# Layer B of a hybrid decoder step: decay rows by a transfer, keys and values turned by VectorE and five transfers instead of TensorE

## The reference, cut to what matters

```python
gc = jnp.cumsum(to_chunks(g, C, N), axis=-1)              # decay logs
diff = gc[..., :, None] - gc[..., None, :]
decay = jnp.where(tri, jnp.exp(jnp.where(tri, diff, 0.0)), 0.0)
kb = kc * bc[..., None]
lmat = jnp.where(strict, jnp.einsum('nbhik,nbhjk->nbhij', kb, kc) * decay, 0.0)
rhs = jnp.concatenate([vc * bc[..., None], kb * jnp.exp(gc)[..., None]], axis=-1)
sol = lax.linalg.triangular_solve(lmat, rhs, left_side=True, lower=True, unit_diagonal=True)
u, w = sol[..., :dv], sol[..., dv:]
aqk = jnp.einsum('nbhik,nbhjk->nbhij', qc, kc) * decay
kdec = kc * jnp.exp(g_last[..., None] - gc)[..., None]

def step(S, xs):
    u_i, w_i, aqk_i, qg_i, kdec_i, gl_i = xs
    v_new = u_i - jnp.einsum('bhck,bhkv->bhcv', w_i, S)
    o_i = jnp.einsum('bhck,bhkv->bhcv', qg_i, S) + jnp.einsum('bhij,bhjv->bhiv', aqk_i, v_new)
    S = S * jnp.exp(gl_i)[..., None, None] + jnp.einsum('bhck,bhcv->bhkv', kdec_i, v_new)
    return S, o_i
```

## Time and profile before

| | before |
|---|---|
| median of 3 runs | 2109.37 us |
| the profiled execution, time | 2113.68 us |
| the profiled execution, span | 2111.6 us |
| mean granted clock of TensorE | 0.993 |
| TensorE busy | 2072.5 us |
| VectorE busy | 997.2 us |
| ScalarE busy | 697.7 us |
| GpSimd busy | 454.6 us |
| bytes moved by DMA | 210.34 MB |

### The profile page before, as it was taken

How to read it: one execution, slowest core, us unless ns; L and a number is a source line. 1 busy time by engine, 2 the same in 40 slices (tenths; PEclk the granted TensorE clock), 3 DMA queues, 4 the chain that set the end, 5 groups by cost and what they waited for, 6 DMA issues and landing times. The chain is left out here.

```text
span 2111.6 us, 36594 instructions
## 1 busy us (share of the span) xinstructions
PE 2072.5 (98%) x14446; PEld 1487.2 (70%) x14446; DVE 997.2 (47%) x2664; ACT 697.7 (33%) x1631; POOL 454.6 (22%) x639
## 2 busy tenths in 40 slices
PE   8999999999999999999999999999999999999998
PEld 6888888888888887555466777767666666665444
DVE  5234354354435345331238777777876133332252
ACT  4121321322131122231135555555564344532101
POOL 0522232222223213300023134322331200020000
PEclk9999999999999999999999999999998999999999
DMA  7411301211131127668412122222210461134451
GB/s 235 161 43 41 107 27 51 80 41 43 41 97 37 50 83 223 237 202 255 131 31 74 73 95 83 93 87 82 73 48 13 137 256 31 41 105 134 134 161 50
DMA packets 210238, 210.34 MB, mean 100 GB/s; under 512 B 14261, under 2 KB 181653, under 8 KB 209150
## 3 DMA queue, kind: packets, MB, share of 16 engines
q1 hardware_dynamic: 198070, 148.27, 23.7%
q0 software_dynamic: 12000, 59.73, 7.4%
HBM read 179.56 MB, written 68.23 MB: 117 GB/s over the span
## 5 line engine op out<-in xcount | busy, mean ns | idle before, releaser
L887 PE MATMUL bank<-arena 128*128 128x256 f32 (+1 forms) x2688 | 631.7, 386 | 0.0
L887 PEld LDWEIGHTS bank<-arena 128*128 128x128 f32 x2688 | 494.5, 190 | 75.3
L2104 PE MATMUL bank<-arena 128*128 128x352 f32 x1296 | 452.5, 470 | 0.1
L2104 PEld LDWEIGHTS bank<-arena 128*128 128x128 f32 x1296 | 220.8, 191 | 71.4 <-issue 1.0
L2909 PE MATMUL bank<-arena 128*128 128x352 f32 x576 | 176.4, 459 | 0.0
L3399 PE MATMUL bank<-arena 128*128 128x512 f32 x360 | 167.5, 599 | 0.0
L2162 PEld LDWEIGHTS bank<-arena 128*128 128x128 f32 x864 | 129.9, 194 | 45.7 <-DVE arena L2646 3.7
L2909 PEld LDWEIGHTS bank<-arena 128*128 128x128 f32 x576 | 106.6, 190 | 53.3
L1341 POOL TENSOR_TENSOR arena<-arena 128x272 f32<-128x272 f32 (+1 forms) x48 | 31.5, 656 | 507.4 <-ACT arena L1061 487.4
L2162 PE MATMUL bank<-arena 128*128 128x128 f32 x864 | 135.0, 280 | 1.5 <-DVE arena L2646 1.0
L1323 POOL TENSOR_TENSOR arena<-arena 128x512 f32<-128x512 f32 x96 | 122.8, 1279 | 11.3 <-POOL arena L1323 0.9
(11 more groups left out here) (432 smaller groups left out, 2754.1 us busy)
## 6 DMA issues: line engine op xcount, KB each, us to landing
arena<-in_w_in_a SPq DMA_DIRECT2D x48, 512.0 KB, 5.2
arena<-in_w_in_b SPq DMA_DIRECT2D x40, 512.0 KB, 7.5
arena<-in_cache_win_k SPq DMA_DIRECT2D x48, 256.0 KB, 6.1
arena<-in_cache_win_v SPq DMA_DIRECT2D x48, 256.0 KB, 4.7
out<-arena SPq DMA_DIRECT2D x40, 256.0 KB, 3.4
arena<-in_w_mem_kv SPq DMA_DIRECT2D x16, 512.0 KB, 8.1
arena<-in_cache_mem_k SPq DMA_DIRECT2D x32, 256.0 KB, 4.3
arena<-in_cache_mem_v SPq DMA_DIRECT2D x32, 256.0 KB, 4.2
```

Source lines behind the costliest of these rows:

```text
L887: m = nc.tensor.matmul(o[:, 0:hi - lo], w, y, start=k == 0 and i in (0, 1, 3, 5), stop=k == KH - 1, skip_group_check=i in (2, 4, 6))
L2104: m = nc.tensor.matmul(bank[j % 3][:, 0:PART], ring.slots[:, (B1 + b) % RING, k, :], part_in(k, part_), start=k == 0, stop=k == KD - 1)
```

## The change

It takes three kinds of transposition off TensorE.

- **Decay rows.** Ahead of the loop TensorE turns all 64 columns of decay logs once (`decay_rows`), VectorE copies the result, and SP stores it in DRAM (`gc_kept`). For each group but the first SP loads its four rows from there, broadcast to all partitions, an iteration ahead into a buffer of their own (`rows_to`). VectorE adds the mask from there in slot 5 (`mask_rows`).
- **Keys and values.** In slots 6 and 7 VectorE turns the keys and values of group G + 1 in 32x32 blocks in SBUF (`kv_turned`). One transfer puts both into DRAM, four bring them back with the blocks in their final places (`turned_away`, `turned_back`). ScalarE scales them into `kdec` and `vb` in slots 8 to 11 of the next iteration, two activations per chunk (`scale_turned`; slots 5 to 8 for the last group).
- **Order.** `PREP` loses `ra`, `kt` and `vt`; SP's list is written per iteration; iteration 15 has its 20 units later. The `Chain` semaphores, so far never freed, are now freed at the end of each phase.

```diff
+    turned_kept = dram("turned_kept", [2, P, 1024])
+    gc_kept = dram("gc_kept", [64, P])
...
+    gc_rows = r_sb[0:64, 1, :]
...
+    turned_in = [brT[:, HB - 2, 0:1024]] * (2 * HB - 1) + [xpad[:, 0, 0:1024]]
+    turned_kv = [w.rearrange("p (b i c x) -> p b i c x", b=4, i=2, c=4) for w in turned_in]
+    kv_words = sb[:, ZM[0]:ZM[0] + 1024]
+    kv_back = kv_words.rearrange("p (a i c x) -> p a i c x", a=4, i=2, c=4)
+    rows_of = [sb[:, MQ[0]:MQ[0] + 512]] * (2 * HB - 1) + [xpad[:, 1, 0:512]]
...
-    PREP = {5: ("ra",), 7: ("kt",), 8: ("kk",), 9: ("qk",), 15: ("vt",)}
-    NEXT = ("ra", "kk", "qk")
+    PREP = {8: ("kk",), 9: ("qk",)}
+    NEXT = ("kk", "qk")
+    AT_MASK = 5
...
+    AT_TURN = {6: 0, 7: 1}
+    scale_at = lambda G: 5 if G == 2 * HB - 1 else 8
...
-    slots += [[(0, 1)] * 16, [(0, 2)] * 4 + [(0, 1)] * 12]
+    slots += [[(0, 1)] * 16, [(0, 0)] + [(0, 1)] * 10 + [(0, 2)] * 5]
...
+        def rows_to(g):
+            h, c0 = g // 2, GR[g % 2][0]
+            sp.wait_ge(rows_away, 16)
+            after(sp, masked, g - 1)
+            if g == NG_ - 1:
+                sp.wait_ge(cvd, 3 * NG_)
+                sp.wait_ge(tap, 3 * (NG_ - 2))
+            src = gc_kept.rearrange("(c h) i -> h c i", h=HB)[h, c0:c0 + 4]
+            sp.dma_start(rows_of[g], src.unsqueeze(0).to_broadcast([P, 4, P])).then_inc(rows_in, 16)
+        def turned_away(g):
+            sp.wait_ge(turnd, 2 * (g + 1))
+            sp.dma_start(turned_kept[g % 2], turned_in[g]).then_inc(kv_away, 16)
+        def turned_back(g):
+            sp.wait_ge(kv_away, 16 * (g + 1))
+            after(sp, kvs, 4 * g)
+            src = turned_kept[g % 2].rearrange("(a y) (b m) -> b y a m", a=4, b=4)
+            for b in range(4):
+                sp.dma_start(kv_words[quarter(b)].rearrange("p (a m) -> p a m", a=4), src[b]).then_inc(kv_in, 16)
...
+        for G in range(NG_):
+            if G % 2 and G < NG_ - 1:
+                weights(3 * (G // 2) + 8)
+                weights(3 * (G // 2) + 9)
+            if G + 2 < NG_:
+                rows_to(G + 2)
+            if G + 1 < NG_:
+                turned_away(G + 1)
+                turned_back(G + 1)
+            if G % 2 == 0:
+                weights(3 * (G // 2) + 7)
...
-                readout(pe, g, f"ks{c}" if c else "vt")
+                if c:
+                    readout(pe, g, f"ks{c}")
+                else:
+                    pe.wait_ge(kvs, 4 * g + 1)
...
+                pe.wait_ge(kvs, 4 * g + cl + 1)
...
+        def scale_turned(g, cl):
+            w, c = hd[:, g // 2 % 2], GR[g % 2][0] + cl
+            if not cl:
+                act.wait_ge(kv_in, 64 * (g + 1))
+                act.wait_ge(hdv, 3 * g + 3)
+                if g > 1:
+                    left(act, g - 2, f"su{GR[g % 2][1] - 1}")
+            wide = lambda v: v.rearrange("p (a x) -> p a x", x=32)
+            nc.scalar.activation(wide(kdec[:, c, :]), kv_back[:, :, 0, cl, :], ACT.Copy, scale=w[:, KD_, c:c + 1])
+            nc.scalar.activation(wide(vb[:, c, :]), kv_back[:, :, 1, cl, :], ACT.Copy,
+                                 scale=w[:, KN, c:c + 1]).then_inc(kvs, 1)
...
-            elif name == "kt":
-                dve.wait_ge(hdv, 3 * G + 3)
-                nc.vector.tensor_tensor(kdec[:, cs, :], bk(b), factors_of[:, KD_, cs].unsqueeze(2)
-                                        .to_broadcast([P, 4, P]), ALU.mult).then_inc(rd_dve, 1)
-            elif name == "vt":
-                nc.vector.tensor_tensor(vb[:, cs, :], bk(b), factors_of[:, KN, cs].unsqueeze(2)
-                                        .to_broadcast([P, 4, P]), ALU.mult).then_inc(rd_dve, 1)
+        def kv_turned(G, i):
+            h, gr = G // 2, G % 2
+            dve.wait_ge(sild, 3 * G + 2 + i)
+            if G and not i:
+                dve.wait_ge(kv_away, 16 * G)
...
+            x = qkvT[:, h % 2, 1 + i, gr * 512:(gr + 1) * 512].rearrange("p (c b x) -> p c b x", c=4, b=4)
+            nc.vector.transpose(turned_kv[G][:, :, i].rearrange("p b c x -> p c b x"), x).then_inc(turnd, 1)
+        def mask_rows(G):
+            dve.wait_ge(rows_in, 16 * G)
+            if G > 2:
+                left(dve, G - 3, f"av{GR[(G - 3) % 2][1] - 1}")
+            nc.vector.tensor_tensor(ATs[G % 3], rows_of[G], wide4(mat(M_GE)), ALU.add).then_inc(masked, 1)
```

More of the change, by code:

```diff
@@ L525, in _ @@
     def _(dve):
-        own = Chain(nc, dve, "in_dve")
+        own = Chain(sem, dve, "in_dve")
         def norm(n):
@@ L1130, in _ @@
     def _(dve):
-        own = Chain(nc, dve, "dve_a")
+        own = Chain(sem, dve, "dve_a")
         def evacuate(t, i):
@@ L1300, in _ @@
     def _(pool):
-        own = Chain(nc, pool, "pool_a")
+        own = Chain(sem, pool, "pool_a")
         def weight_sums(pair, ns):
@@ L1747, in _ @@
     def _(dve):
-        own = Chain(nc, dve, "wa_dve")
+        own = Chain(sem, dve, "wa_dve")
         def add(n, half):
@@ L2078, in state_away, with weights @@
             sp.dma_start(p_delta[0, 0, h], S_of(h, NT)).then_inc(s_out, 16)
-        for b in range(3 * HB):
+        def rows_to(g):
[16 more added lines that the diff above has]
+                sp.dma_start(kv_words[quarter(b)].rearrange("p (a m) -> p a m", a=4), src[b]).then_inc(kv_in, 16)
+        def weights(b):
             if b % 3 == 2 and b // 3 >= 3:
@@ L2082, in _ @@
             ring.load(sp, B1 + b + 1)
-        state_away(HB - 3)
-        ring.load(sp, B2 + RING)
+        for b in range(7):
+            weights(b)
+        readout(sp, 0, "gr")
+        sp.dma_start(gc_kept, gc_rows).then_inc(rows_away, 16)
+        rows_to(1)
+        turned_away(0)
+        turned_back(0)
+        for G in range(NG_):
[9 more added lines that the diff above has]
+                weights(3 * (G // 2) + 7)
         state_away(HB - 2)
@@ L2313, in gate_piece @@
                 act.wait_ge(ring.used, B2 + i + 1)
+            if i == 0 and part_ == 0:
+                act.wait_ge(masked, NG_ - 2)
+            if i == 1 and part_ == 0:
+                act.wait_ge(kvs, 4 * NG_)
             if i == 2 and part_ == 0:
@@ L2379, in exps @@
         def exps(G):
-            readout(act, G, "ra")
+            if G:
+                act.wait_ge(masked, G)
+            else:
+                readout(act, 0, "ra")
             act.wait_ge(hdv, 3 * G + 2)
@@ L2489, in _ @@
     def _(dve):
-        own = Chain(nc, dve, "b_dve")
+        own = Chain(sem, dve, "b_dve")
         stepped = [0]
@@ L2735, in _ @@
         turned(0, "qk")
+        kv_turned(0, 0)
+        kv_turned(0, 1)
         for w in range(CW):
@@ L2742, in _ @@
             for s in SLOTS:
+                if s == AT_MASK and G + 1 < NG_:
+                    mask_rows(G + 1)
                 if G < NG_:
@@ L2746, in _ @@
                     chunk_step(G - 1, s)
+                if s in AT_TURN and G + 1 < NG_:
+                    kv_turned(G + 1, AT_TURN[s])
                 if s == AT_INV:
@@ L2772, in _ @@
     def _(pool):
-        own = Chain(nc, pool, "b_pool")
+        own = Chain(sem, pool, "b_pool")
         def prefix(h, i):
@@ L3009, in _ @@
     def _(dve):
-        own = Chain(nc, dve, "m_dve")
+        own = Chain(sem, dve, "m_dve")
         def conv_turned(t):
@@ L3487, in _ @@
     def _(act):
-        own = Chain(nc, act, "d_act_own")
+        own = Chain(sem, act, "d_act_own")
         def squared(o):
@@ L3558, in _ @@
     def _(dve):
-        own = Chain(nc, dve, "wb_dve")
+        own = Chain(sem, dve, "wb_dve")
         gt2 = lambda v: v[:, 64:66].unsqueeze(2)
```

33 lines of the change are left out of this document (23 added, 10 removed).

## The result

The changed kernel takes 2274.43 us (median of 4 runs, 2271.98 to 2277.12), the kernel before 2111.76 in the same session (4 runs): ratio 1.077, 95% interval 1.075 to 1.080, 163 us slower.

The account below looks back on a forecast made before the run. TensorE's own instruction list was taken to bound layer B's loop in iterations 1 to 12. +0.8 ahead of it, -9.7 in it and -1.0 in the last iterations sum to -9.9 us: 2099.5 us from 2109.37, range 2091 to 2107.

Parts of the forecast that it names:

- the transfers: SP's queue, each iteration: 512 KB out, four of 128 KB back, 256 KB of decay rows; claimed to cost nothing.
- the rivals: Every four counts in full, 2088.7 us, 7%; gain mostly given back, 2105 to 2109, 19%; clock, 8%; slower, 6%.
- slower: Rival, 6%: VectorE's transposition ahead of L2562 costs 2.17 us and not 0.71, delaying answers to TensorE; about 2125 us.
- The clock rival: Layer B: a second half-clock stretch of TensorE, 2104.5 us, or the present one gone, 2094.5 us; 8%.
- SP's transfers landing after slot 8: One of the signs listed beforehand that would show the forecast wrong, in the loop; no size given.
- What leaves TensorE: Slots 5, 7 and 15: three fours of transpositions at 0.44 us leave TensorE, 1.32 us per iteration.
- What TensorE runs into: Level-4 products after slot 7: a new 0.51 us wait for VectorE's base transposition; net gain 0.81 per iteration, 9.7 over twelve.
- The addition: VectorE's decay-row addition in slot 5, now from SBUF: about 0.69 us, nothing lost; other end +2.5 us from waits for GpSimd.
- VectorE's transpositions: Slots 6 and 7: two of 128x512 at 0.71 us each, covered by VectorE's 1.76 us wait for ScalarE's exponentials.
- ScalarE's pairs: From slot 8, four slots: two activations each, 0.78 us per slot; 1.0 us of cover at the first, so costed at nothing.
- Ahead of the loop: Before the loop: two transpositions delay the first level-4 products by 1.3 us, slot 15 gives 0.44 back: +0.8 us.
- The last iterations: Iterations 13 to 15: TensorE already waits or nearly waits at level 4, so together -1.0 us, ends 0 and -2.

Follow-up runs that it names:

- e8: The changed kernel with cache copies in 16 pieces per batch and VectorE's decay-row addition moved from slot 5 to slot 7: 2098.71 us, ratio 0.994.
- e1: The changed kernel without the twelve cache copies GpSimd issues in layer B's loop, their outputs not written: 2102.24 us, ratio 0.995.
- e2: The changed kernel with the same cache copies cut into 16 pieces per batch, outermost dimension 16 and not 2: 2106.40 us, ratio 0.997.
- e9: The changed kernel with only decay rows by transfer, keys and values turned on TensorE as before, copies in 16 pieces: 2110.98 us, ratio 0.999.
- e10: The changed kernel with only keys and values by VectorE and transfers, decay rows on TensorE as before, copies in 16 pieces: 2104.73 us, ratio 0.996.
- e6: The changed kernel with only keys and values by VectorE and transfers, decay rows on TensorE as before, copies as given: 2255.24 us, ratio 1.068.
- e7: The changed kernel with each cache copy split into two transfers, its even and odd pieces of about 2 KB: 2184.88 us, ratio 1.034.

## Why the prediction was wrong

**The step that failed** is the one on the transfers: "A near size, 520 KB back from DRAM, lands in 3.9 us", so "Nothing", and the rows and copies are "needed almost an iteration later". The 3.9 us of the earlier trace rows are from a part of the kernel in which no cache copy runs. Beside the copies of layer B's loop the 512 KB out took up to 59.1 us to land (median over the loop 29.2), more than the 34 of an iteration. It was not a term that was mis-sized a little: I priced a transfer by its size and looked at what SyncE has in its list, not at what else the DMA engines have. The trace of before had the signs, unused: GpSimd's copies of 2 MB run all through the loop, and beside them the profile gives, for 1130 to 1640 us:

```profile
arena<-in_w_in_b SPq DMA_DIRECT2D x22, 512.0 KB, 10.2
```

Weights of 512 KB on SyncE's own queue landed after 10.2 us in the median, not 3.9, and after 42 to 44 in each of the five cases from 1156.9 to 1429.0 us in which a head's third block was asked for; this with the DMA share at 0.27. The step also took SyncE's waits to be those for ring slots. The change adds two that hang on the late landing: the way back stands behind the landing of the way out in SyncE's list, and VectorE's next transposition waits for the same landing, since there is one staging buffer. None of the rivals held it; "slower" was built on a transposition of 2.17 us. In the list of what would show the forecast wrong, "SP's transfers landing after slot 8" is what came. The clock rival was right that idle time brings half clock, but it is a consequence here, 28 of the 163 us at most: 7.8 us more busy time, and 20 us of transpositions that should have left it.

**What leaves TensorE**: 1.32 us an iteration. Right: e8, in which nothing gives it back, gains 1.31.

**What TensorE runs into**: a wait of 0.51, net 0.81. Right: 0.43 measured in e1, net 0.79 in e2, and over the twelve iterations e1 is 9.8 us shorter (9.7 forecast). e9 and e10 fit as well: slot 5's four buys 0.35 (0.43 expected), the other two 0.81 (0.87 expected), and all three in place 0.79.

**The addition** at 0.69: measured 0.69 (mean of fifteen in e8). In slot 5, its place in e1 and e2, the longest of fifteen took 0.73 and 0.74, so the wait for GpSimd that was the other end (+2.5) did not come.

**VectorE's transpositions** at 0.71: measured 0.70, and the wait for the exponentials went from 1.76 to 1.19 (forecast about 1.0). **ScalarE's pairs** were costed at nothing: right, TensorE did not wait for ScalarE's copy in the loop of e1.

**Ahead of the loop** the forecast was +0.8: too much. TensorE does wait 1.19 us at its first level-4 products in e2, but they start at 1131.35, only 0.64 later (forecast 1.3) than the 1130.71 of before, and the exponentials of the iteration after come at 1162.58, before's at 1162.63.

**The last iterations** were forecast at -1.0. From the last exponentials of the loop to the end, before takes 510.95 us, e1 513.25, e2 513.4, so +2.3; e1 has 2.2 less in the iteration ahead of it (half clock for 6.8 us in place of 13.7), e2 has not. Why the end is longer was not tried.

**The sum**: with the transfers free of the copies, e1 takes 2102.24 and e2 2106.40 against a forecast of 2099.5 with a range of 2091 to 2107. Against before in the same session that is a gain of 10.5 and 6.4 us; 9.9 was forecast. The parts on the engines were about right, in the loop by their mechanism. That e1's sum comes so near is in part luck: its start is 2.3 us better than the term (the exponentials of iteration 1 come at 1161.12) and its last iterations are 1.1 worse. The kernel as changed is 163 us slower.

## What to carry to other kernels

Before a wait is hung on a transfer, look at its landing times next to everything else in flight in that stretch, the largest value and not the median, and at the copies that "cost nothing". A copy between DRAM tensors whose outermost dimension is 2 held two DMA engines for 40 to 42 us here: put a dimension of 16 outermost (one line here), and only then move work from an engine to transfers. With that line and the addition two slots later this change is worth 0.6% (e8, 2098.7 us); as it stood, it lost 7.7%.

## What the runs showed of the hardware

- Two queues with work on the same DMA engine took turns of one packet, whatever its size: 13 packets of 65,024 bytes (2.40 us each) to 13 of 4096 (0.16 us) in 16 us of after, on two engines. A transfer of 256 KB in 512 pieces took 41 us beside a copy, 4.8 without.
- The issue itself can be held, and with it all that stands behind it in the list: SyncE's issue of the way out took 32.75 us in after, with a late rows transfer ahead of it, at most 0.34 in e6, which has no rows, and at most 1.1 in e2. What holds it the records don't show.
- The packets of a copy of 2 MB took 40 to 42 us, on two engines, with its outermost dimension 2; with 16 it landed in 8.5 us, and the spread copies slow the others' landings little: 4.6 against 3.6 us for the way out in e2 and e1.
- Cutting a copy into pieces of 2 KB moved the cost to GpSimd, which stood up to 28.1 us ahead of an issue (e7).
- Half clock follows idle time: 181 us of it in layer B in after, 13.7 in before and e2, 6.8 in e1 and e8.
